# Row broadcasts between two halves of a projection; sums of squares in four column groups; one weight slot loaded outside the ring

## What is computed

```python
def rms_norm(x, g):
    y = xf * lax.rsqrt(jnp.mean(xf * xf, axis=-1, keepdims=True) + RMS_EPS)
def layer_norm(x, g, b):
    var = jnp.mean(jnp.square(xf - mu), axis=-1, keepdims=True)
    return (xf - mu) * lax.rsqrt(var + LN_EPS) * g + b
```

## Time and profile before

| | before |
|---|---|
| median of 3 runs | 2236.47 us |
| profiled execution, its own time | 2235.85 us |
| its span | 2234.1 us |
| PE busy | 1999.6 us (90%) |
| DVE busy / ACT busy / POOL busy | 590.4 / 420.9 / 204.9 us |
| mean granted TensorE clock | 0.964 of 2.4 GHz |
| moved by DMA | 664.24 MB, 297 GB/s over the span |

### The profile page before, as it was taken

The page is one execution under the profiler, slowest core; times in us unless marked ns, Lnnn a source line. Parts: engine busy times, 40 slices in busy tenths (PEclk is TensorE's granted clock), DMA queues, the critical chain, the costliest instruction groups (busy, mean ns, idle before and its releaser), DMA issues.

```text
span 2234.1 us, 32626 instructions
## 1 busy us (share of the span) xinstructions
PE 1999.6 (90%) x14110; PEld 1407.8 (63%) x14110; DVE 590.4 (26%) x1172; ACT 420.9 (19%) x772; POOL 204.9 (9%) x183
## 2 busy tenths in 40 slices
PE   8989998876887888987888887999999999999997
PEld 4856675642455456653565443856888887588886
DVE  5655410114412000000001102454432034640001
ACT  3222221211312000000001211434200033630001
POOL 0830000001000000000000000324000003700000
PEclk9999999998999999998999998999999999999999
DMA  9938799999999999999999999531586743044450
GB/s 369 364 147 350 294 425 406 418 423 426 393 414 426 427 426 423 423 421 426 425 416 425 426 397 369 138 114 39 187 297 216 184 142 104 11 151 151 127 155 19
DMA packets 181383, 664.24 MB, mean 297 GB/s; under 512 B 17432, under 2 KB 121401, under 8 KB 142649
## 3 DMA queue, kind: packets, MB, share of 16 engines
q1 hardware_dynamic: 181240, 662.15, 75.7%
HBM read 661.08 MB, written 1.05 MB: 296 GB/s over the span
## 4 chain that ended last, share of the span: by engine, by line
PE 47%; DMA 22%; DVE 3%; ACT 3%; issue 1%; SPq 0%; ACTq 0%; POOL 0%; DVEq 0%; POOLq 0%
PE ps L1180 19%; PE ps L679 10%; DMA ring<-in_context_weights 8%; DMA ring<-in_w_gate 7%; DMA ring<-in_w_down_slots 5%; PE ps L1619 4%; DMA ring<-in_w_up 3%; PE ps L1016 2%; PE ps L1645 2%; PE ps L1189 2%; PE ps L980 2%; ACT arena L2553 1%; PE ps L875 1%; PE ps L1658 1%; PE ps L705 1%
## 5 line engine op out<-in xcount | busy, mean ns | idle before, releaser
L1180 PE MATMUL ps<-arena,ring 128*128 128x256 f32 x1984 | 429.9, 380 | 1.0 <-DVEq L391 0.9
L1180 PEld LDWEIGHTS ps<-arena,ring 128*128 128x128 f32 x1984 | 377.2, 190 | 53.5 <-issue 1.7
L1619 PE MATMUL ps<-ring,arena 128*32 128x256 f32 x4032 | 259.5, 404 | 80.2 <-DMA ring<-in_w_gate 42.2
L679 PE MATMUL ps<-arena,ring 128*128 128x256 f32 (+2 forms) x1372 | 310.6, 387 | 9.1 <-DMA ring<-in_context_weights 8.9
L679 PEld LDWEIGHTS ps<-arena,ring 128*128 128x128 f32 (+2 forms) x1372 | 250.0, 188 | 75.0 <-DMA ring<-in_context_weights 25.7
L1619 PEld LDWEIGHTS ps<-ring,arena 128*32 128x32 f32 x4032 | 126.5, 115 | 199.1 <-DMA ring<-in_w_gate 51.0
L2260 ACT ACTIVATE arena<-ps 128x512 f32<-128x512 f32 (+3 forms) x143 | 76.6, 536 | 737.5 <-PE ps L679 330.8
L1645 PE MATMUL ps<-ring,arena 128*32 128x512 f32 x1024 | 141.6, 676 | 63.1 <-DMA ring<-in_w_down_slots 55.1
L1645 PEld LDWEIGHTS ps<-ring,arena 128*32 128x32 f32 x1024 | 29.9, 118 | 154.7 <-DMA ring<-in_w_down_slots 88.7
L3068 POOL TENSOR_TENSOR XC<-XC,arena 128x256 f32<-128x256 f32 x32 | 23.4, 730 | 983.7 <-ACT XC L2354 963.5
L3078 POOL TENSOR_SCALAR arena<-arena 128x512 f32<-128x512 f32 x48 | 78.3, 1631 | 88.1 <-DVE arena L2973 84.7
(11 more groups left out here) (375 smaller groups left out, 2014.8 us busy)
## 6 DMA issues: line engine op xcount, KB each, us to landing
ring<-in_w_up SPq DMA_DIRECT2D x64, 2048.0 KB, 13.3
ring<-in_w_down_slots SPq DMA_DIRECT2D x64, 2048.0 KB, 14.3
ring<-in_w_gate SPq DMA_DIRECT2D x62, 2048.0 KB, 13.8
ring<-in_w_ada SPq DMA_DIRECT2D x28, 2048.0 KB, 9.2
ring<-in_w_ffn_in SPq DMA_DIRECT2D x44, 1024.0 KB, 7.7
ring<-in_context_weights SPq DMA_DIRECT2D x35, 1024.0 KB, 14.7
ring<-in_w_ffn_out SPq DMA_DIRECT2D x16, 1408.0 KB, 7.0
ring<-in_w_in SPq DMA_DIRECT2D x9, 2048.0 KB, 11.2
```

Source lines behind the costliest of these rows:

```text
L679: m = mm(o, a, x, start=(k == 0 and r == 0), stop=(k == kt - 1 and last))
L1180: m = mm(b, w[:, k, c:c + P], src[:, k, :], start=(k == 0), stop=(k == kt - 1))
L1619: m = mm(b[u][32 * c:32 * c + 32, T * x:T * x + T], xs[:, 2 * h + k, CAP * e:CAP * e + CAP], w[:, k, at_:at_ + T], start=(h == 0 and k == ...
```

## The change

Four edits:

1. `token_rows(1, "arow")` moves from behind `project("x2")` to between its halves.
2. `ss1`, `ssf`, `lv0` and `lv1` of the latent tokens (the context keeps the old form) are summed in four column groups: tile `k` goes through 32 columns of ones into partitions 32 (k mod 4) and up. ACT copies the bank to SBUF, and one product with the full matrix of ones folds the four groups and broadcasts (each sum is then 32 times too large, and the root's scale has 1/32). Between sums and fold stand, on PE: at `ss1` one `ada` step, at `ssf` four k-steps of a raw tile, at `lv0` and `lv1` of layer 0 two k-steps, at the last `lv1` nothing.
3. The modulation slot ada0_11 is loaded to arena column 16424, once the scores are weighted (`p_ready`), instead of into the ring. Expert tile gate0_0, which goes to the same place, waits for its use.
4. With one slot less in the ring, each later load that goes to the ring lies elsewhere and waits for another tile: before, ada1_0 to ada1_3 waited for out1, ada0_7, ada0_8 and ada0_11, now for out0, out1, ada0_7 and ada0_8; 30 of the loads behind them, up to the second FFN slot of the context, also have another predecessor. Each new bank shifts the rotation of the banks behind it.

```diff
-        early |= {n: {"ada0_9": 5120, "ada0_10": 0}[name] for n, (name, _) in enumerate(stream) if name in ("ada0_9", "ada0_10")}
+        dead = {"ada0_9": 5120, "ada0_10": 0, "ada0_11": 16424}
+        early |= {n: dead[name] for n, (name, _) in enumerate(stream) if name in dead}
+        in_queries = [name for name, _ in stream].index("ada0_11")
...
+            def group_sums(name, tile, sem, counts):
+                b = open_bank(pe, name + "_part")
+                for k in range(KD):
+                    pe.wait_ge(sem, counts(k))
+                    c = 32 * (k % 4)
+                    m = mm(b[c:c + 32, 0:T], ones[:, 0:32], tile(k), start=(k < 4), stop=(k >= 4))
+                close_bank(m, name + "_part")
+
+            def groups_folded(name, part):
+                bank, use = place[name + "_part"]
+                pe.wait_ge(free[bank], use + 1)
+                b = open_bank(pe, name)
+                close_bank(mm(b[:, 0:T], ones, part, start=True, stop=True), name)
...
@@ raw_queries
-                    b = open_bank(pe, "ssf")
-                    for k in range(KD):
-                        pe.wait_ge(csq_ready[X], k + 1)
-                        m = mm(b[:, 0:T], ones, T1[:, T * k:T * k + T], start=(k == 0), stop=(k == KD - 1))
-                    close_bank(m, "ssf")
+                    group_sums("ssf", lambda k: T1[:, T * k:T * k + T], csq_ready[X], lambda k: k + 1)
                 raw_tile(f"rq0x{l}", w, 0, 2 * l, range(4))
                 if mean:
                     mean(1, KD - 1)
+                else:
+                    groups_folded("ssf", rs)
                 raw_tile(f"rq0x{l}", w, 0, 2 * l, range(4, KD))
                 raw_tile(f"rq1x{l}", w, P, 2 * l)
                 if mean:
-                    variance(X, 1, l - 1, f"x{l - 1}", ALL_BANKS)
-                raw_tile(f"rq2x{l}", w, 2 * P, 2 * l)
+                    latent_variance(1, l - 1)
+                raw_tile(f"rq2x{l}", w, 2 * P, 2 * l, range(2))
+                if mean:
+                    groups_folded(f"lv1x{l - 1}", rs2)
+                raw_tile(f"rq2x{l}", w, 2 * P, 2 * l, range(2, KD))
...
@@ latent
-                variance(X, 0, l, N, ALL_BANKS)
-                raw_tile(f"rb0{N}", w, T, 2 * l + 1)
+                latent_variance(0, l)
+                raw_tile(f"rb0{N}", w, T, 2 * l + 1, range(2))
+                groups_folded(f"lv0{N}", rs2)
+                raw_tile(f"rb0{N}", w, T, 2 * l + 1, range(2, KD))
...
                     mean(1, KD - 1)
-                    variance(X, 1, l, N, ALL_BANKS)
+                    latent_variance(1, l)
+                    groups_folded(f"lv1{N}", rs2)
...
-            project("x2")
-            token_rows(1, "arow")
+            project("x2", between=lambda: token_rows(1, "arow"))
...
@@ router norm, PE (the sums in four groups as above, then)
+            ada()
+            bank, use = place["ss1_part"]
+            pe.wait_ge(free[bank], use + 1)
+            b = open_bank(pe, "ss1", MIX_BANKS)
+            close_bank(mm(b[:, 0:T], ones, rs, start=True, stop=True), "ss1")
+            ada(3)
...
@@ seam, ACT
+                b = read_bank(act, "ssf_part")
+                step(a(rs, b[:, 0:T], ACT.Copy), frees="ssf_part")
                 raw_operand(0, 4)
                 b = read_bank(act, "ssf")
-                step(a(rs, b[:, 0:T], ACT.Sqrt, scale=1.0 / D, bias=tb("eps")), frees="ssf")
+                step(a(rs, b[:, 0:T], ACT.Sqrt, scale=1.0 / (32 * D), bias=tb("eps")), frees="ssf")
                 tell(root_ready)
                 for m in range(5, KD):
                     raw_operand(0, m)
...
@@ SP
+                if stream[n][0] == "ada0_11":
+                    sp.wait_ge(p_ready, 1)
                 load(n)
...
                 if n == n_before:
                     sp.wait_ge(h_ready, 2)
+                    sp.wait_ge(*freed[in_queries])
```

More of the change, by code:

```diff
@@ L1372, in _, with project @@
             T1v = T1.rearrange("p (a b) -> p a b", b=T)
-            def project(n):
+            def project(n, between=None):
                 w = take(n)
@@ L1378, in project @@
                     fmajor(f"{n}{i}", w, 2 * i, lambda k: hT[:, k, :])
+                    if i == 0 and between is not None:
+                        between()
                 release_with(f"{n}1")
@@ L1833, in root @@
             def root(name):
+                b = read_bank(act, name + "_part")
+                step(a(rs, b[:, 0:T], ACT.Copy), frees=name + "_part")
                 b = read_bank(act, name)
-                step(a(rs, b[:, 0:T], ACT.Sqrt, scale=1.0 / D, bias=tb("eps")), frees=name)
+                step(a(rs, b[:, 0:T], ACT.Sqrt, scale=1.0 / (32 * D), bias=tb("eps")), frees=name)
                 tell(root_ready)
```

14 lines of the change are left out of this document (9 added, 5 removed).

## The result

| | before | with the change |
|---|---|---|
| median | 2236.47 us (5 runs, 2231.55 to 2239.99) | 2223.54 us (5 runs, 2222.99 to 2228.26) |
| profiled execution, its own time | 2235.85 | 2222.99 |
| its span | 2234.1 | 2221.2 |
| PE busy | 1999.6 | 1991.9 |
| mean granted TensorE clock | 0.964 | 0.966 |

The ratio is 0.9945, 95% interval 0.9929 to 0.9962. The forecast was 2221.7 with a range of 2217.5 to 2226.5. The execution profiled is 12.9 us shorter where 14.7 were forecast.

What follows compares the result with a forecast made beforehand. Bound by PE and DVE in the front, PE to about 330 us, DMA to 1380, then PE with the norms. 8.2 + 0.1 + 2.5 + 4.1 + 1.9 - 1.0 - 1.05 = 14.7 us won: 2221.7, range 2217.5 to 2226.5.

Steps and rivals of the forecast that it cites:

- Edit 1, 8.2: Front, ahead of z_spectrum(0): 8.2 us won, 5.8 from DVE starting earlier and 2.36 from the clock staying up.
- that rival: Ahead of z_spectrum(0): the clock falls in the small hole too, so 12.3 us are won, 2224.0; chance 0.17.
- Router norm, +0.1: At ss1: root later, at about 253.7, yet PE reaches the logits at about 261.2 against 261.30; worth 0.1 us.
- one of my own signs of being wrong: Front to router norm: the forecast is wrong if PE waits elsewhere in 103 to 260 us.
- The slot, 2.5: Early load of ada0_11, ahead of the experts: 2.5 us won, bounds 1.1 to 4.
- what is left when PE again waits for DMA: Early slot's lead in the experts, from 346.47: 7.4 + 1.1 - 4.5 - 1.5 = 2.5 us.
- The subtraction of gaps: Early slot: 4.5 us of lead lost in an empty queue before the tables, about 1.5 more ahead of gate1_2.
- lv0, 4.1: At lv0, twice: PE is the path and saves 2.04 us each, together 4.1.
- lv1 of layer 0, 1.9: At lv1 of layer 0: root 1.16 us earlier and L705's 0.71 us bank wait gone, together 1.9.
- Seam, -1.0: At ssf: root at 1393.4 instead of 1391.30, PE waits for the last late raw tile; 1.0 us slower.
- Last lv1, -1.05: At the last lv1: copy, fold and hand-overs lie bare and grouping saves nothing; 1.05 us slower.
- The 30 re-placed loads at nothing: Ring loads with new predecessors: no cost, as each has 4.2 MB (10 us) or more queued ahead.

Runs made afterwards that it cites:

- e1: Kernel before with only the transposes of token_rows(1) moved between the halves of x2; median 2228.24 us, ratio 0.9972.
- e2: Changed kernel with ada0_11 loaded through the ring again and the ring's places those of before; median 2227.93 us, ratio 0.9968.
- e13: Changed kernel with the rotation of the banks set one back behind the seam's fold, nothing else; median 2229.00 us, ratio 0.9986.
- e11: As e5, with the bank rotation skipping one bank behind the first half of the first raw query tile; median 2225.04 us, ratio 0.9955.
- e6: Changed kernel with ACT at the router norm evacuating the modulation row's bank ahead of the root; median 2223.16 us, ratio 0.9956.
- e4: Changed kernel with the seam norm ssf back in its one-bank form; median 2224.45 us, ratio 0.9954.
- e5: Changed kernel with ssf, ss1 and the last lv1 back in the one-bank form; median 2227.52 us, ratio 0.9974.
- e8: Changed kernel with ssf and the last lv1 in one-bank form and the router norm as in e6; median 2226.03 us, ratio 0.9957.
- e12: As e8, with the bank rotation skipping one bank behind the first half of the first raw query tile; median 2220.24 us, ratio 0.9937.

## Why the prediction came out right, and where its steps did not

The forecast median, 2221.7, lies 1.8 and 2.4 us under the two that were measured. The gain, forecast at 14.7 us, was 12.9 and 10.7. Put together from what the runs showed, it is 5.8 to 6.8 for edit 1, -0.4 for the router norm, 1 to 4.6 for the slot, and 3.8 + 1.8 - 1.8 - 1.15 for the other norms: 9.1 to 13.7 us. The mechanisms of edit 1 and of the layer norms were right. Edit 1 was put some 2 us too high and the norms together 1.8 (4.05 against 2.25). The slot's term may have made up for part of this or not, so how near the total came says nothing about that term, and in so far it is luck.

- **Edit 1, 8.2.** In the change's profile 7.55. DVE's run began 5.50 us earlier and its last read 5.16; the row's 2.39 came as said. But I read PE's arrival from one profile and took the hole's 1.6 us for a property of the edit. The hole is what is left between PE and DVE, and PE arrived at 109.2 to 110.2 in the six profiles where the clock fell and at 112.0 to 115.2 in the others, because the stretch before was later or the first half of x2 took 8.6 to 8.8 us instead of 7.15. In half of the profiles the hole is 2.6 us and more and the clock falls; that rival had 0.17 and came in 6 of 12. Over all of them the edit is worth about 6, near the lower end of my bounds. (The 95.82 that I took for x2's start is where the view begins; x2 starts at 95.09, which moves the transposes by 0.4 us and not the sum.)
- **Router norm, +0.1.** -0.4 where the clock stays, -2.0 in the change's profile. The root came at 5.01 us behind the first sum, as worked out (253.7 less 248.72). The step that failed is the row bank behind it, whose evacuation waits for the root: I had PE at the logits at 261.2 and did not work out when that bank comes free. The step that needs it started 6.68 us behind the first sum instead of 6.28, behind a wait of 1.77 us instead of 0.81, and I had no term for what the clock may do behind a hole of that length. A wait of PE between 103 and 260 was one of my own signs of being wrong, and here it came.
- **The slot, 2.5.** PE's own wait, 0.9 to 1.3, came. The rest, "what is left when PE again waits for DMA", did not: at 340.84 PE waited 2.70 us, longer than in the earlier trace rows, and stood 5.63 us ahead of before, less than at the tables (6.04). gate0_0 was issued at 261.18 and the tables at 307.68, where I had 258 and 304.5. The subtraction of gaps was right in kind (the empty queue of about 3 us is there) and left a remainder smaller than the experts' draw of several us. What I missed is that PE's own wait is no fixed price: it was 0.90 in before, 1.28 in e1 and 4.6 in e2, as PE's steps ahead of it ran. Its worth in the change is therefore open between 1 and 4.6 us.
- **lv0, 4.1.** 1.9 twice. **lv1 of layer 0, 1.9.** 1.8, with both parts: the root 1.2 earlier and no bank wait at L707.
- **Seam, -1.0.** -1.84 against the form with one bank at the same clock. I let PE wait for the last of the raw tiles 5 to 7 and not for the first, which it reaches a k-step behind the fold; the fold's 0.43 and about 1.4 of waiting and later starts add up, and nothing takes them back.
- **Last lv1, -1.05.** -1.15.
- **"The 30 re-placed loads at nothing"**: no run shows a price. **"Each new bank shifts the rotation"**: I counted the 0.71 us it gave and not what it could take. With the rotation one bank back, 5 to 8 us of the gain would have been lost (e13). The prediction works out a bank for L705's counterpart alone. That the rank product's fell well too was in no sum and in no rival, and was luck.

The norm part of the forecast rested on the three places where two k-steps stand beside the copy, and there it held. The Trainium skill (TensorEngine Tiling (Array Packing), section "PSUM Bottleneck") says that tiling speeds up TensorE but not the evacuation, which may become the bottleneck. Here the new form lost at three places of six (router, seam, last norm: -0.4, -1.84, -1.15) and won at the other three (1.9, 1.9 and 1.8). What decided was how much PE had to do beside the copy and who waited for the root.

## What to carry to other kernels

Where banks are handed out in rotation, every bank that an edit adds or removes changes which earlier tile each later product waits for: list for the first product behind each norm who read its bank last, before believing any difference that an edit makes elsewhere. A form that wins PE time and adds an evacuation paid only where PE had as much other work as the copy took and nothing else stood behind the root, so it is decided place by place. A transfer made early is worth the wait that it removes, and that wait changes from execution to execution with how soon PE gets there: look at several profiles before pricing it. And where runs of one kernel spread by ten microseconds, two medians of a dozen runs do not tell 3 us apart.

## What the runs showed of the hardware

- The clock behind a hole. Holes up to 1.82 us ahead of `z_spectrum(0)` left it at 2.4 GHz in six profiles, holes from 2.60 us brought it to 1.2 GHz for the next row in six. That makes no rule, for at other places the same hole does both. Behind 1.77 us a step took 1.92 in four profiles and 3.22 in one, behind 2.48 us (2.47 in two) 1.92 in five and 2.57 to 3.64 in nine. What else decides is open.
- One fall may bring another. Some 50 us behind the rank product of layer 0 PE waits 1.8 to 2.4 us on its own issue; the next row takes 3.72 us or 5.1 to 5.4. It took the longer time in all six profiles with the grouped seam and in two of eight with the other, and these two (before, e11) had the row ahead of the seam at the lower clock (5.74 and 6.68 us for the combination instead of 3.69; 5.72 in e6, which is grouped). So the grouped seam may cost 1.7 us more than its 1.84, and between 1380 and 1579 e4, e5, e8 and e12 do gain 3.9 to 4.3 us where the change gains 0.6. No run tests this alone.
- The same instructions behind the tables, bound by DMA at a share of 1.00, took 1063.6 to 1070.9 us (1066.65 before), and the first 90 us, ahead of every edit, differed by 4.8 us between profiles. Both are as large as the effects looked for; only short stretches between two named rows told effects of 2 us apart.
